# Branch and output products of a hybrid encoder layer in one block, and a second norm that works tile by tile

## The reference, cut to what matters

```python
g_ssm, g_attn = jnp.split(jax.nn.sigmoid(gates), 2, axis=-1)
merged = g_ssm * (y_ssm @ w_branch_ssm) + g_attn * (o @ w_branch_attn)
x = x + gate1 * (merged @ w_out)
h2 = rmsnorm(x, norm2_g) * (1 + scale2) + shift2
x = x + gate2 * peer_ffn(h2, peer_wq, peer_keys, peer_u, peer_v)
```

## Time and profile before

| | us |
|---|---|
| three runs, median (lowest to highest) | 5283.17 (5282.93 to 5286.81) |
| the profiled execution, its own time | 5286.62 |
| its span in the profile | 5284.8 |
| TensorE busy | 4614.6 (87%) |
| VectorE busy | 3585.1 (68%) |
| ScalarE busy | 1782.7 (34%) |
| GpSimd busy | 1520.9 (29%) |

### The profile page before, as it was taken

The page is one execution under the profiler, slowest core; times in us unless marked ns, Lnnn a source line. Parts: engine busy times, 40 slices in busy tenths (PEclk is TensorE's granted clock), DMA queues, the critical chain, the costliest instruction groups (busy, mean ns, idle before and its releaser), DMA issues. The chain is left out here.

```text
span 5284.8 us, 83802 instructions
## 1 busy us (share of the span) xinstructions
PE 4614.6 (87%) x28787; PEld 4259.7 (81%) x28787; DVE 3585.1 (68%) x6877; ACT 1782.7 (34%) x3697; POOL 1520.9 (29%) x1356
## 2 busy tenths in 40 slices
PE   5999999788887969875888576999999999999995
PEld 3999999677775549874788466999999999999994
DVE  3011555454554641234699996999999999999996
ACT  3111333223232641111344594333333333333332
POOL 0000000111110000000000002677777777777772
PEclk7999999888897889987999798999999999999997
DMA  3332222222222232342699457999999999999995
GB/s 134 126 136 85 80 93 89 112 106 105 104 107 74 54 110 93 131 157 85 258 350 330 182 191 268 352 362 368 367 364 369 369 359 366 368 361 367 369 363 195
DMA packets 349646, 1170.31 MB, mean 221 GB/s; under 512 B 40001, under 2 KB 91329, under 8 KB 342081
## 3 DMA queue, kind: packets, MB, share of 16 engines
q0 software_dynamic: 147456, 536.94, 27.3%
q1 hardware_dynamic: 159328, 483.07, 25.7%
q10 hardware_dynamic: 42720, 148.52, 7.4%
HBM read 971.20 MB, written 197.46 MB: 221 GB/s over the span
## 5 line engine op out<-in xcount | busy, mean ns | idle before, releaser
L2042 POOL DMA_INDIRECT ex_vr<-in_expert_v,ex_at x512 | 649.4, 1268 | 232.6 <-issue 149.9
L2040 POOL DMA_INDIRECT ex_ur<-scr_u_rows,ex_at x512 | 596.3, 1165 | 311.4 <-DVE ex_ur L2217 130.8
L2225 DVE SCALAR_TENSOR_TENSOR ex_acc_rows<-ex_vr,ex_wt,ex_acc_rows 128x1024 f32<-128x1024 f32 x512 | 649.2, 1278 | 43.1 <-ACT ex_wt L2145 37.3
L2217 DVE SCALAR_TENSOR_TENSOR ex_ur<-ex_ur,h_rows 128x1024 f32<-128x1024 f32 x512 | 619.1, 1218 | 14.6 <-DMA ex_ur<-scr_u_rows,ex_at 14.6
L2034 POOL COPY ex_at<-picked_at 128x4 uint32 x128 | 70.2, 549 | 1617.8 <-POOLq L121 1617.3
L897 POOL TENSOR_TENSOR sd_cts<-sd_cT,sd_ea 128x512 f32<-128x512 f32 x72 | 92.2, 1281 | 1521.1 <-ACT sd_ea L855 1521.1
L2052 PE MATMUL ex_ps<-hd_hi,ex_u_hi 128*128 128x320 f32 x2048 | 470.6, 311 | 30.2 <-DVE ex_u_lo L2191 27.7
L2052 PE MATMUL ex_ps<-hd_lo,ex_u_hi 128*128 128x320 f32 x2048 | 468.4, 310 | 0.0
L2052 PE MATMUL ex_ps<-hd_hi,ex_u_lo 128*128 128x320 f32 x2048 | 468.3, 310 | 0.0
L2143 ACT ACTIVATE ex_gel<-ex_dot 128x1 f32<-128x1 f32 x512 | 103.9, 203 | 996.5 <-DVE ex_ur L2217 996.5
L447 DVE TENSOR_TENSOR pr_w_lo<-pr_w,pr_w_hi 128x1024 fp32r<-128x1024 f32 x58 | 71.1, 1225 | 509.0 <-ACT pr_w_hi L443 509.0
(11 more groups left out here) (381 smaller groups left out, 11409.4 us busy)
## 6 DMA issues: line engine op xcount, KB each, us to landing
pk_raw_u<-in_expert_u SPq DMA_DIRECT2D x128, 512.0 KB, 6.5
scr_u_rows<-pk_rows_u ACTq DMA_DIRECT2D x128, 512.0 KB, 6.2
ex_u<-in_expert_u SPq DMA_DIRECT2D x128, 512.0 KB, 7.1
ex_v<-in_expert_v SPq DMA_DIRECT2D x128, 512.0 KB, 9.6
scr_gate<-gt_stage SPq DMA_DIRECT2D x10, 4096.0 KB, 13.8
ex_gate<-scr_gate SPq DMA_DIRECT2D x32, 1280.0 KB, 9.0
pr_w<-in_w_main SPq DMA_DIRECT2D x58, 512.0 KB, 4.5
scr_xbc<-pr_out ACTq DMA_DIRECT2D x32, 576.0 KB, 3.7
```

Source lines behind the costliest of these rows:

```text
L2040: nc.gpsimd.indirect_dma_start(out=ur[:, s], out_offset=None, in_=scr["u_rows"], in_offset=by).then_inc(ur_in[s], 16)
L2042: nc.gpsimd.indirect_dma_start(out=vr[:, s], out_offset=None, in_=io["expert_v"].rearrange("j i d -> (j i) d"), in_offset=by).then_inc(vr_ ...
L2217: v.scalar_tensor_tensor(out=ur[:, s], in0=ur[:, s], scalar=1.0, in1=rows[:, s], op0=ALU.mult, op1=ALU.mult, accum_out=dot[:, m:m + 1]).th ...
L2225: v.scalar_tensor_tensor(out=acc_g[:, s], in0=vr[:, s], scalar=wt[:, m:m + 1], in1=acc_g[:, s], op0=ALU.mult, op1=ALU.add).then_inc(row_r[ ...
```

## The change: what it does

`phase_merge` and `phase_out` with their three uses of `phase_split_product` are replaced by one block, `phase_branches`, with four products `j` of eight slices each: the first and the second half of the SSM branch, the attention branch and the output product. There are two operand sets: `x[0]` for j = 0 and 2, `x[1]` for j = 1 and 3. While the tiles of product j run (j = 0, 1), one operand tile of product j + 1 per output tile is loaded, rounded and its remainder taken. Weights have two buffers for what is loaded (`w_new[:, s]`), the extras still one.

The half sum of j = 0 is copied from PSUM by ScalarE and stored as `branch`. Product j = 1 adds it to its PSUM and multiplies by the gate, and the result is stored as `merged`. Product j = 2 multiplies by its gate, adds `merged`, and its result does not go to DRAM: ScalarE rounds it into `x[1][0]` and VectorE writes the remainder into `x[1][1]`, the operand of j = 3. Product j = 3 does what "ou" did; x1 is still stored. In j = 3 ScalarE also squares each tile and VectorE adds the squares up; after the last tile TensorE sums over the partitions (nine one-column products), and the reciprocal root of each token stays on chip as `rs2` (128 x 9).

`phase_norm2` no longer computes the sums. TensorE spreads `rs2` over the row, and each tile of x1 is worked on when its own transfer has landed. The wide scaling and the two casts move from VectorE to ScalarE.

The diff, its core (removed lines are those of the functions printed above; `open_gate`, `round_weights`, `rest_of_weights`, `store` are as before apart from the counts they wait for; `finish` of j = 2 and 3 as in "ma" and "ou"; in `tiles` TensorE goes through j, then m, in loops of three rounds of two and two more written out):

```diff
...
+def phase_branches(nc, io, per, scr):
...
+        x = [[sb(f"br_x{n}_{part}", [P, KD, T], F32R) for part in ("hi", "lo")] for n in range(2)]
+        w = [sb(f"br_w_{part}", [P, 2, KD, P], F32R) for part in ("hi", "lo")]
+        w_new, x_new = sb("br_w_new", [P, 2, KD, P]), sb("br_x_new", [P, 2, T])
+        ex, out, g1 = sb("br_extras", [P, 2, T]), sb("br_out", [P, 2, T]), sb("br_gate", [P, 2, NC_])
...
+        sq, total = x_new[:, 0], x_new[:, 1]
...
+            def load_weights(j, i, s):
+                sp.wait_ge(w_lo[s], i + j * HALF_T + START)
+                sp.dma_start(w_new[:, s], weights[j](i * 2 + s).rearrange("m p k c -> p (m k) c")).then_inc(w_in[s], 16)
+            def load_operand(j, k):
+                n = j * KD + k
+                if n >= 2:
+                    sp.wait_ge(x_lo, n - 1 + START)
+                sp.dma_start(x_new[:, n % 2], sources[j](k)).then_inc(x_in[n % 2], 16)
+            def load_extras(j, i, s):
+                sp.wait_ge(done[1 - s], i + ((j - 1) * HALF_T + s) + START)
+                if j < 3:
+                    sp.wait_ge(stored[s], i * 16 + (STORES[j - 1] + 1) * 16 + START)
+                for n, tile in enumerate(extras[j](i * 2 + s)):
+                    sp.dma_start(ex[:, n], tile).then_inc(ex_in[s], 16)
+            load_weights(0, 0, 0)
+            for k in range(KD):
+                load_operand(0, k)
+                if k == 1:
+                    load_weights(0, 0, 1)
+            for j in range(4):
+                for m in range(MT):
+                    i, s = m // 2, m % 2
+                    if j > 0:
+                        load_extras(j, i, s)
+                    if m + 2 < MT:
+                        load_weights(j, i + 1, s)
+                    elif j < 3:
+                        load_weights(j + 1, 0, s)
+                    if j < 2:
+                        load_operand(j + 1, m)
...
+            def round_operand(j, k):
+                n = j * KD + k
+                act.wait_ge(x_in[n % 2], n // 2 * 16 + 16 + START)
+                if j == 2:
+                    for s in range(2):
+                        act.wait_ge(mm[s], HALF_T + START)
+                nc.scalar.copy(x[j % 2][0][:, k], x_new[:, n % 2]).then_inc(x_hi, 1)
...
+            for j in range(4):
+                for m in range(MT):
+                    i, s = m // 2, m % 2
+                    if j in (1, 2):
+                        open_gate(j, i, s)
+                    if j < 2:
+                        round_operand(j + 1, m)
+                    if m + 2 < MT:
+                        round_weights(j, i + 1, s)
+                    elif j < 3:
+                        round_weights(j + 1, 0, s)
+                    if j == 0:
+                        act.wait_ge(mm[s], i + 1 + START)
+                        act.wait_ge(stored[s], i * 16 + START)
+                        nc.scalar.copy(cut(out[:, s]), banks(ps[:, s])).then_inc(scaled[s], 1)
+                        act.wait_ge(scaled[s], i + 1 + START)
+                        store(scr["branch"], i, s)
+                        continue
+                    act.wait_ge(done[s], (j - 1) * HALF_T + i + 1 + START)
+                    if j == 1:
+                        store(scr["merged"], i, s)
+                    elif j == 2:
+                        for e in range(2):
+                            act.wait_ge(mm[e], 2 * HALF_T + START)
+                        nc.scalar.copy(x[1][0][:, m], out[:, s]).then_inc(m_hi, 1)
+                    else:
+                        store(scr["x1"], i, s)
+                        if m >= 2:
+                            act.wait_ge(added, m - 1 + START)
+                        nc.scalar.activation(total if m == 0 else sq, out[:, s], ACT.Square).then_inc(squared, 1)
+            act.wait_ge(summed, 1 + START)
+            nc.scalar.activation(per["rs2"][:], vps[:, 0:NT], ACT.Sqrt, bias=per["eps"][:, 0:1], scale=1.0 / D).then_inc(rooted, 1)
...
+            def step(j, i, s, after):
+                pe.wait_ge(w_lo[s], i + (j * HALF_T + 1) + START)
+                pe.wait_ge(scaled[s], i + j * HALF_T + START)
+                for k in range(KD):
+                    if j < 3:
+                        pe.wait_ge(x_lo, j * KD + k + 1 + START)
+                    else:
+                        pe.wait_ge(m_lo, k + 1 + START)
+                    for a, b in SPLIT:
+                        for c in range(3):
+                            last = nc.tensor.matmul(ps[:, s, c, 0:CW], w[a][:, s, k], x[j % 2][b][:, k, c * CW:(c + 1) * CW],
+                                                    start=(k == 0 and (a, b) == SPLIT[0]), stop=(k == KD - 1 and (a, b) == SPLIT[-1]))
+                last.then_inc(mm[s], 1)
+            tiles(pe, step)
+            pe.wait_ge(added, MT - 1 + START)
+            for t in range(NT):
+                last = nc.tensor.matmul(vps[:, t:t + 1], total[:, t * P:(t + 1) * P], ones[:, 0:1], start=True, stop=True)
+            last.then_inc(summed, 1)
...
+            def add_squares(m):
+                dve.wait_ge(squared, m + 1 + START)
+                if m > 1:
+                    dve.wait_ge(added, m - 1 + START)
+                v.tensor_tensor(total, total, sq, ALU.add).then_inc(added, 1)
...
+                if j == 1:
+                    v.tensor_tensor(cut(out[:, s]), banks(ps[:, s]), cut(ex[:, 1]), ALU.add).then_inc(scaled[s], 1)
+                    dve.wait_ge(scaled[s], n + 1 + START)
+                    v.tensor_tensor(out[:, s], out[:, s], ex[:, 0], ALU.mult).then_inc(done[s], 1)
...
+                if j == 2:
+                    dve.wait_ge(m_hi, m + 1 + START)
+                    v.tensor_tensor(x[1][1][:, m], out[:, s], x[1][0][:, m].bitcast(F32), ALU.subtract).then_inc(m_lo, 1)
...
+            for j in range(4):
+                for m in range(MT):
+                    i, s = m // 2, m % 2
+                    if j < 2:
+                        rest_of_operand(j + 1, m)
+                    if m + 2 < MT:
+                        rest_of_weights(j, i + 1, s)
+                    elif j < 3:
+                        rest_of_weights(j + 1, 0, s)
+                    if j > 0:
+                        finish(j, i, s)
+                    if j == 3 and m >= 2:
+                        add_squares(m - 1)
+            add_squares(MT - 1)
+            dve.wait_ge(rooted, 1 + START)
+            v.reciprocal(per["rs2"][:], per["rs2"][:])
...
+            for t in range(NT):
+                last = nc.tensor.matmul(rps[:, t * P:(t + 1) * P], per["rs2"][:, t:t + 1].to_broadcast([P, P]), ident, start=True, stop=True)
+            last.then_inc(spread_r, 1)
             for k in range(KD):
...
+            def keep(k):
+                act.wait_ge(turned, k + 1 + START)
+                nc.scalar.copy(rows[:, :, k * P:(k + 1) * P], pst[:, k % 2]).then_inc(kept, 1)
+            for k in range(KD):
+                b = k % 2
+                act.wait_ge(normed, k + 1 + START)
+                if k >= 2:
+                    act.wait_ge(rest, k - 1 + START)
+                    act.wait_ge(turned, k - 1 + START)
+                nc.scalar.activation(out[:, b, 0:SEQ], x[:, k, 0:SEQ], ACT.Identity, scale=gain[:, k, 0:1], bias=mod[:, shift_at + k, 0:1]).then_inc(scaled, 1)
+                act.wait_ge(scaled, k + 1 + START)
+                act.wait_ge(moved, k + 1 + START)
+                nc.scalar.copy(hd[0][:, k], out[:, b, 0:TD])
+                nc.scalar.copy(hg[0][:, k], out[:, b, TD:T]).then_inc(made, 1)
+                if k > 0:
+                    keep(k - 1)
+            keep(KD - 1)
...
+            def move(k):
+                b = k % 2
+                dve.wait_ge(x_in[k], 16 + START)
+                v.tensor_tensor(x[:, k], x[:, k], rps[:, 0:T], ALU.mult).then_inc(normed, 1)
+                dve.wait_ge(normed, k + 1 + START)
+                if k >= 2:
+                    dve.wait_ge(rest, k - 1 + START)
+                    dve.wait_ge(turned, k - 1 + START)
+                ch.link(v.tensor_tensor(samples(out[:, b]), samples(x[:, k]), per_token(gain, k), ALU.mult))
+                v.tensor_tensor(samples(out[:, b]), samples(out[:, b]), per_token(mod[:, shift_at:shift_at + KD], k), ALU.add).then_inc(moved, 1)
+            move(0)
             for k in range(KD):
                 b = k % 2
+                if k + 1 < KD:
+                    move(k + 1)
                 dve.wait_ge(made, k + 1 + START)
                 v.tensor_tensor(hd[1][:, k], out[:, b, 0:TD], hd[0][:, k].bitcast(F32), ALU.subtract)
+                v.tensor_tensor(hg[1][:, k], out[:, b, TD:T], hg[0][:, k].bitcast(F32), ALU.subtract).then_inc(rest, 1)
...
```

More of the change, by code:

```diff
@@ L1298, in _ @@
         @block.sync
         def _(sp):
[L1300 to L1317, removed]
-                    load_weights(i + 1, s)
-            for s in range(2):
-                load_extras(KD // 2 - 1, s)
+            def load_weights(j, i, s):
```

(23 more changed lines are left out.)

193 lines of the change are left out of this document (83 added, 110 removed).

## The result

| | before | after |
|---|---|---|
| median of four runs, us (lowest to highest) | 5284.68 (5282.93 to 5286.81) | 5164.22 (5161.86 to 5167.07) |
| the profiled execution, its own time, us | 5286.62 | 5167.07 |
| first transfer of the block to that of the picks, us | 599.4 | 488.8 |

The ratio of after to before is 0.9772 (95% interval 0.9755 to 0.9789): 120.5 us less between the medians, where 100 was forecast.

The account below looks back on a forecast made before the run. TensorE's matmuls, 12.5 us a tile, were the floor, with operand loading, seams and the second norm leaving it not full. Terms -81.4 + 25 + 4 - 48 = -100.4 us took 5286.6 to 5186, as a median 5183; range 5155 to 5210.

Parts of the forecast that it names:

- the rival that the round does not bind: Middle products: slices land early or the lag is absorbed; stalls 0 to 3 us, gain 125, time 5158; chance 0.19.
- seams: Starts of the SSM, attention and output products: loading and empty stretches beyond arithmetic mostly go, -81.4 us together.
- stalls behind them, clock included: Products j = 1 to 3: TensorE waits of 16.3 and 5.4 us plus 3 for the clock, 25 us (0 to 40).
- end of the block: After the last tile of j = 3: last square, add, sums, root and reciprocal lengthen it by about 4 us (0 to 7).
- second norm: Stretch from the block to the picks: 88.7 us before, 40.6 after, 48 saved (40 to 52).
- the rival that it would not run on: Instruction order holds the next operand until a product ends: three seams cost 18 us each, time 5212; chance 0.03.
- Stalls in j = 1: Second product: a round takes 16.1 us against 12.5 for a tile, stalling from tile 5; gives back 16.3 us.
- Stalls behind it: Products j = 2 and 3: rounds of 12.5 us (11.3 to 13.3) in j = 2, then a 5.4 us stall in j = 3.
- The clock: Behind TensorE's gaps in the middle products and j = 3: matmuls at the low clock cost 3 us.
- The rival with the low clock through the middle products: TensorE stays at 1.2 GHz in j = 1 and 2: all sixteen tiles cost 168 us, time 5326; chance 0.03.
- the head: Start of the second norm: row spread of 2.27 us beside the first x1 tile's flight, 7 us (5 to 9).
- the rival of the longer round: Second product: slice after 11.5 us, rounds of 18 us; gain 75, time 5208; chance 0.19.

## Why the prediction was right

The way and most of the sum came out as put on record; the median is 19 us below the forecast, and the sign by which the forecast would be wrong (not about 499 us from the block's first transfer to the picks') was missed by 10: 488.8. By the time alone the rival that the round does not bind (5158) is nearer than the forecast (5183). The trace decides between them.

| term of the sum | forecast, us | measured in the block's trace, us |
|---|---|---|
| seams (loading beyond arithmetic: 100.9 before, 20.4 after) | -81.4 | -80.5 |
| stalls behind them, clock included (1.9 before, 16.5 after) | +25 | +14.6 |
| end of the block | +4 | +6.6 |
| second norm | -48 | -51.3 |
| sum | -100.4 | -110.6 |

**Seams.** The loading to the second tile was put at 32 us and took 32.9. TensorE ran on at j = 1 without a gap; the rival that it would not run on fell, and putting one seam back cost 17.5 us of the 18 that this rival gave it.

**Stalls in j = 1.** The round was forecast at 16.1 us, with ScalarE's cast of a late slice in it: 15.5 to 16.3, mean 15.9. The forecast's 64.6, 80.7, 96.8, 112.9 came as 64.1, 80.0, 96.0, 112.1, and the second tile of j = 2 at 127.7 for 129.0. Without the stall it would have begun at 112.3 (nine tiles of 12.48), so j = 1 gave back 15.4 us for 16.3. Against the rival that the round does not bind, whatever its time, stand these gaps, and the 12.1 us that came back when the slice was issued first.

**Stalls behind it: the term that was mis-sized.** I took 12.5 us for a round of j = 2, the middle of 11.3 to 13.3; it was 11.8 on average, and the wait at j = 3 was 0.6 us for 5.4. The two extras took 5.4 us from the first issue to the sigmoid, where the bounds came from 4.85 (one extra beside a store) and 6.78 (two beside a store): without the store the round lies 0.5 us above the lower bound, with it, at 13.3, on the upper. The page DMA: Bandwidth & Descriptors of the Trainium skill, section Issuing engines are not separate DMA queues, says that what SP and ScalarE issue runs on the same 16 engines and interleaves; the trace agrees, with 6.9 us beside the store for 5.4 without it. I had the right bounds, and a mechanism that spoke for one end, and took the middle.

**The clock.** 3 us were put beside the other stalls. In j = 1 they are already inside the 15.4: the four gaps are 9.9 us, two small waits in the first tile of j = 2 are 1.2, the slow matmuls behind the gaps of 3.15 and 3.38 us are 3.1 (1.65 and 1.45), and the rest is handoffs. The 1.65 fill the wait of their own round, as the forecast has it, so that only the 1.4 behind the last gap lengthen anything. At j = 3 the wait is only 0.6 us, the three matmuls behind it take 0.80, and there was nothing to pay. (Nor were 4.5 us lost in the earlier trace rows: nearly 9 us at 0.96 for 0.52 lose 4.0.) The rule on the page TensorE: Matmul & The Clock Gate of the Trainium skill, section HAM oscillation, that a wait for data starts the next group of matmuls slow, holds in part: behind the gap of 3.38 us three matmuls take 1.33 us at once; behind that of 3.15 they turn slow after a microsecond (2130.31); behind the two near 1.7 us, shorter waits than those of the page's example, they stay at full pace. The rival with the low clock through the middle products fell: 0.94 is the lowest clock of a stretch there.

**End and norm.** The last square does not directly follow the last tile (done by 2368.55): there is one buffer for squares, and VectorE still adds the former one until 2369.81. That is 1.3 of the 2.6 us by which the end was put too low. From the reciprocal's end (2377.02) to the next block's first row are 2.9 us, where the forecast's terms leave 1.8 (7.9 + 4 - 3 - 7.1): 1.1 more. The rest is handoffs.

In the norm the head took 6.4 us (2379.96 to 2386.36) for 7, but not by the mechanism put on record. The forecast had it set by the flight of the first tile, with a spread of 2.27 us beside it. Measured are 2.4 us for the constants and 4.0 for the spread, at a granted clock of 0.55 in that stretch; the first tile is there after 4.1 us (with the constants loaded early, 2361.54 to 2365.68). That the sizes agree is luck. Seven rounds took 23.0 us for 24.5, and the end, from VectorE's last row to the next block, 4.1 for 5: with the head 3.0 of the 3.2 us between 40.6 and 37.4.

**Two sums of the rivals.** By its own terms the rival with the low clock turns the gain into a loss from twelve slow tiles on, not ten (12 x 10.5 - 25 = 101), and the rival of the longer round comes to a gain of some 83 us, not 75. The forecast itself rests on neither.

**What lies outside.** 9 of the 120 us belong to no step of the forecast: 15.6 less behind, 6.7 more ahead (but for 0.6 of opening). The runs put the second down to scatter, and up to 10 of the first to where the tensors lie; the rest of it is of the size of the scatter.

## What to carry over

In one SP queue the order of loads is a schedule: the slice that the next chain needs first belongs ahead of the tile that is used last, and that one line gave 12 us of the block in the profile, some 10 of the time. When a bound is open at both ends, ask which mechanism sets it before taking the middle. A second buffer for only the tile that the chain works on first (the gate), on top of that line, brought the round down to TensorE's 12.5 us; it was not run by itself.

## What was not expected of the hardware

- The same program with 64 bytes more in front of its later tensors ran all from the picks on in 2752.8 us instead of 2763.5 and 2763.8, with nothing computed otherwise; only addresses differ. 128 bytes gave 2763.4, and 192 gave 2754.9 but no measurable time.
- Two profiles of one program differ by 6 us in the start of a block 1.9 ms into it (1921.9 and 1927.9).
